# Roots of a norm made token by token, and one accumulated read of a state, in a two-layer decoder step

## The reference, cut to what matters

```python
def rms_norm(x, gain=None):
    y = x * lax.rsqrt(jnp.mean(x * x, axis=-1, keepdims=True) + EPS)
    return y * gain

def decoder_layer(x, ...):
    h = x + 0.5 * rms_norm(swiglu(rms_norm(x, n_ffn1_pre), ffn1_w_in, ffn1_w_out), n_ffn1_post)
    m, ... = token_mixing(rms_norm(h, n_mix_pre), ...)
    h = h + rms_norm(m, n_mix_post)
    h = h + 0.5 * rms_norm(swiglu(rms_norm(h, n_ffn2_pre), ffn2_w_in, ffn2_w_out), n_ffn2_post)
```

## Time and profile before

| what | value |
|---|---|
| median of 3 runs | 1864.43 us (1863.88 to 1865.13) |
| profiled execution, own time | 1863.31 us |
| its span, first to last instruction | 1861.5 us |
| PE busy | 1810.6 us, 97% |
| DVE busy | 1344.2 us, 72% |
| ACT busy | 902.9 us, 49% |
| POOL busy | 118.5 us, 6% |
| chain that ended last | PE 71%, DVE 16%, issue 5%, ACT 4%, DMA 2% |
| DMA | 368.20 MB, mean 198 GB/s |

### The profile page before, as it was taken

One profiled execution on the slowest core, in us unless ns is written; L12 is line 12 of the kernel. 1 busy time (PEld: TensorE's weight loads), 2 busy tenths in 40 slices (PEclk: granted clock), 3 DMA queues, 4 the chain that ended last, 5 costly groups with the idle time before them and its releaser, 6 DMA issues.

```text
span 1861.5 us, 40412 instructions
## 1 busy us (share of the span) xinstructions
PE 1810.6 (97%) x16247; PEld 1746.6 (94%) x16247; DVE 1344.2 (72%) x2096; ACT 902.9 (49%) x1051; POOL 118.5 (6%) x174
## 2 busy tenths in 40 slices
PE   7999999999999999999999999999999899999998
PEld 6999999988989999999999999999889899989998
DVE  6777577787777868877577765868777776887764
ACT  5443354546574254543354434465567545354433
POOL 0000001111210100000000000010112010000000
PEclk9999999999999999999999999999999999999999
DMA  7776666766864656566667766676778465546654
GB/s 231 216 206 192 178 196 221 237 226 216 276 227 139 192 169 220 162 191 168 173 188 212 205 184 198 198 247 201 232 235 283 138 205 170 181 129 189 182 163 133
DMA packets 433619, 368.20 MB, mean 198 GB/s; under 512 B 9395, under 2 KB 411125, under 8 KB 432811
## 3 DMA queue, kind: packets, MB, share of 16 engines
q1 hardware_dynamic: 409560, 276.60, 50.0%
q0 software_dynamic: 23872, 89.03, 14.2%
HBM read 338.90 MB, written 26.69 MB: 196 GB/s over the span
## 4 chain that ended last, share of the span: by engine, by line
PE 71%; DVE 16%; issue 5%; ACT 4%; DMA 2%; DVEq 0%; SPq 0%; ACTq 0%
PE proj L686 46%; PE proj L709 4%; PE proj L704 4%; PE proj L705 4%; DVE wl L1859 3%; ACT wh L1364 2%; PE aux L749 1%; PE proj L660 1%; PE aux L919 1%; PE aux L1141 1%; PE aux L864 1%; PE aux L880 1%; DVE y L2053 1%; DVE x L2054 1%; DMA raw<-w_mem_v 1%
## 5 line engine op out<-in xcount | busy, mean ns | idle before, releaser
L1859 DVE TENSOR_TENSOR wl<-raw,wh 128x2048 fp32r<-128x2048 f32 (+1 forms) x280 | 599.2, 2140 | 193.2 <-ACT wh L1364 167.9
L1364 ACT CAST wh<-raw 128x2048 fp32r<-128x2048 f32 (+1 forms) x280 | 500.3, 1787 | 249.3 <-PE proj L686 105.9
L686 PE MATMUL proj<-xl,wh 128*128 128x264 f32 x2624 | 381.4, 286 | 1.9 <-DVEq L2009 1.3
L686 PE MATMUL proj<-xh,wh 128*128 128x264 f32 x2624 | 380.1, 287 | 0.0
L686 PE MATMUL proj<-xh,wl 128*128 128x264 f32 x2624 | 372.0, 284 | 1.8 <-DVE wl L1859 1.1
L686 PEld LDWEIGHTS proj<-xl,wh 128*128 128x128 f32 x2624 | 341.3, 188 | 15.5 <-issue 13.2
L686 PEld LDWEIGHTS proj<-xh,wl 128*128 128x128 f32 x2624 | 339.0, 188 | 4.2 <-DVE wl L1859 3.9
L686 PEld LDWEIGHTS proj<-xh,wh 128*128 128x128 f32 x2624 | 340.0, 188 | 3.1 <-issue 0.8
L705 PE MATMUL proj<-hl,wh 128*128 128x264 f32 x704 | 173.3, 283 | 0.0
L704 PE MATMUL proj<-hh,wh 128*128 128x264 f32 x704 | 173.0, 283 | 0.0
L1385 ACT ACTIVATE gate<-gate 128x264 f32<-128x264 f32 x88 | 37.4, 425 | 246.2 <-DVEq L1895 246.2
(11 more groups left out here) (477 smaller groups left out, 2271.5 us busy)
## 6 DMA issues: line engine op xcount, KB each, us to landing
raw<-ffn_w_in SPq DMA_DIRECT2D x176, 512.0 KB, 5.1
raw<-w_in SPq DMA_DIRECT2D x80, 1024.0 KB, 5.6
raw<-ffn_w_out SPq DMA_DIRECT2D x64, 704.0 KB, 4.6
sring<-cache_mem_k POOLq DMA_DIRECT2D x32, 512.0 KB, 5.1
sring<-cache_mem_v POOLq DMA_DIRECT2D x32, 512.0 KB, 4.0
out<-sring POOLq DMA_DIRECT2D x32, 512.0 KB, 4.5
sring<-state_gdn POOLq DMA_DIRECT2D x30, 512.0 KB, 5.1
raw<-w_mem_v SPq DMA_DIRECT2D x8, 1024.0 KB, 6.9
```

What stands on the lines that cost most here:

```text
L686: mm = pe.matmul(o, w[:, s, k * 256 + t * P:k * 256 + (t + 1) * P], a[:, k, :], **go)
L1364: act.copy(wh[:, slot, 0:size], raw[:, slot, 0:size]).then_inc(hi_done[slot], 1)
L1859: dve.tensor_sub(wl[:, slot, 0:size], raw[:, slot, 0:size], wh[:, slot, 0:size].bitcast(F32)).then_inc(split_done[slot], 1)
```

## The change

At three places (layer 0 after `out`, layer 0 after `f2o`, layer 1 after `out`) the sums of squares are made with `acc` as the stationary operand, 128 tokens at a time, against one column of ones: the sum of a token then stands in that token's partition, three tokens a partition. ScalarE takes the roots of 128x3 values, VectorE inverts them and announces `row_roots`. Between that and the multiplications of `y` VectorE does the split that stood in front of `add_result` (only in layer 0's two places). TensorE spreads the three columns over all partitions with three matmuls against the identity, and VectorE multiplies `y` with the roots straight from PSUM.

The delta rule's reads: the stationary operand `gqm` has 128 columns a sample, zero but for the columns of that sample, so that the products of all eight samples add up in one bank (`gd`), which VectorE copies once. TensorE itself releases the states' slots. With it `rn1` moves behind the sixth matmul of the second tile of group 1, and from banks 0 and 1 to 2 and 3; `gQ0` and `gQ1` move from bank 1 to 2; `query_part(1)` moves behind `o_ret`.

```diff
@@ banks, in the order of use
-         + ["gvn1", "gd0", "rn0", "rn1", "gd1", "gbr0", "gG0", "gQ0", "gd2", "gbr1", "gG1", "gQ1", "gd3", "gT"]
+         + ["gvn1", "gd", "rn0", "rn1", "gbr0", "gG0", "gQ0", "gbr1", "gG1", "gQ1", "gT"]
-              "spt": 2, "gvn0": 0, "rd7": 2, "rS6": 0, "rS7": 2, "rdt": 0, "gqd": 1, "gvn1": 2, "gd0": 1, "rn1": 0, "gd1": 2, "gbr0": 0, "gG0": 3, "gQ0": 1,
-              "gd2": 2, "gbr1": 0, "gG1": 3, "gQ1": 1, "gd3": 2, "gT": 0}
+              "spt": 2, "gvn0": 0, "rd7": 2, "rS6": 0, "rS7": 2, "rdt": 0, "gqd": 1, "gvn1": 2, "gd": 1, "rn1": 2, "gbr0": 0, "gG0": 3, "gQ0": 2,
+              "gbr1": 0, "gG1": 3, "gQ1": 2, "gT": 0}
@@ TensorE
+            ENDS = (0, P, T - P)
+            def row_sums(l, name):
+                norm_wait(pe, l, "sqp", int(name[1]))
                 o = begin(l, name)
+                for c, first in enumerate(ENDS):
+                    mm = pe.matmul(o[:, 0, c:c + 1], acc[:, first:first + P], ones[:, 0:1], start=True, stop=True)
+                end(mm, name)
+            def spread_roots(l, n):
+                pe.wait_ge(M["row_roots"], 2 * l + n - 1)
+                o = begin(l, f"r{n}")
+                for c, (first, width) in enumerate(((0, P), (P, P), (SEQ, NS))):
+                    mm = pe.matmul(o[:, 0, first:first + width], mx[:, c:c + 1].broadcast_to([P, P]), ident[:, P - width:P], start=True, stop=True)
+                end(mm, f"r{n}")
...
                 def last_result(g):
                     if l and g == 0:
-                        total(l - 1, "p3", "sqp")
+                        row_sums(l - 1, "p3")
+                def last_roots(g, t, k):
+                    if l and (g, t, k) == (0, 1, 3):
+                        spread_roots(l - 1, 3)
...
                 def read_delta(g, t, k):
+                    if (g, t, k) == (1, 1, 1):
+                        retention_sums(1)
                     if (t, k) != (1, 3):
                         return
-                    o = begin(l, f"gd{g}")
-                    for c in range(2):
-                        unit_wait(pe, l, D_UNIT + 2 * g + c)
-                        mm = four_heads(o[:, 0, c * DV:(c + 1) * DV], lambda h: gqw[:, h, :], delta_unit(2 * g + c), start=True, stop=True)
-                    end(mm, f"gd{g}")
+                    o = begin(l, "gd") if g == 0 else aux[:, PLACE["gd"][0]:PLACE["gd"][0] + 1, :]
+                    for b in (2 * g, 2 * g + 1):
+                        slot = unit_wait(pe, l, D_UNIT + b)
+                        mm = four_heads(o[:, 0, 0:DV], lambda h: gqm[:, b * P + h * 32:b * P + (h + 1) * 32], delta_unit(b),
+                                        start=(b == 0), stop=(b == NS - 1))
...
                     elif g == 1:
                         second("rsq", 1)
-                        for s in range(2):
-                            o = begin(l, f"rn{s}")
...
+                        retention_sums(0)
...
                 else:
                     mixed_result(0)
-                    keep_streaming(l, "n3", 22)
+                    o = begin(l, "n3")
+                    keep_streaming(o, 4)
+                    spread_roots(l, 2)
+                    keep_streaming(o, 11)
@@ ScalarE
+            def row_root(l, name):
+                o = take(act, l, name)
+                order(act.activation(mx[:, 0:3], o[:, 0, 0:3], ACT.Sqrt, bias=epst[:], scale=1.0 / D))
+                release(act, name)
+                act.sem_inc(M["rtp"], 1)
@@ VectorE
-                def add_result(n):
+                def add_result(n, between=None):
                     norm_wait(dve, l, "rtp", n)
-                    order(dve.reciprocal(rt[:], rt[:]))
+                    if n == 1:
+                        root = rt[:]
+                        order(dve.reciprocal(root, root))
+                    else:
+                        order(dve.reciprocal(mx[:, 0:3], mx[:, 0:3]))
+                        tell("row_roots")
+                        if between:
+                            between()
+                        root = take(dve, l, f"r{n}")[:, 0, 0:T]
...
                     elif g in (2, 3):
                         z = g - 2
+                        if g == 2:
+                            ready("rS_out")
+                            order(dve.memset(gqm[:], 0.0))
...
-                        order(cp(gqw[:].rearrange("p h (c n) -> p c h n", c=2), qkvt[:, 0:8, T - 16:T].rearrange("p (c h) n -> p c h n", c=2)))
+                        last = (NS - 1) * (P + 1)
+                        for c in range(2):
+                            own_columns = gqm[:, 0:last].rearrange("p (b j) -> p b j", j=P + 1)[:, :, NS + 16 * c:P:32]
+                            order.apart(cp(own_columns.rearrange("p b h -> p h b"), qkvt[:, 4 * c:4 * c + 4, SEQ:T - 1]))
+                            order.apart(cp(gqm[:, last + NS + 16 * c::32], qkvt[:, 4 * c:4 * c + 4, T - 1]))
+                        order.wait()
...
-                def read_delta(k):
-
-                    o = take(dve, l, f"gd{k}")[:, 0, :]
-                    for c in range(2):
-                        own_part(accd, o[:, c * DV:(c + 1) * DV], own_row, 2 * k + c)
-                    release(dve, f"gd{k}")
...
+                def keep_delta_reads():
+                    order(cp(accd[:], take(dve, l, "gd")[:, 0, 0:DV]))
+                    release(dve, "gd")
+                    dve.sem_inc(unit_used[(D_UNIT + NS - 1) % SRING], 1)
+                    tell("reads")
...
                 def finish_retention(g, remainder=None):
-                    if g < 3:
-                        read_delta(g)
...
-                        read_delta(3)
-                        query_part(1)
+                        keep_delta_reads()
                 def gate_retention(g):
                     if g == 3:
...
                         tell("o_ret")
+                        query_part(1)
```

More of the change, by code:

```diff
@@ L98 @@
          + ["gv0", "gx4", "gS0", "go0", "gks", "gx5", "gv1", "gx6", "go1", "gS1", "gx7", "gm0", "gm1"]
-         + ["p2", "n3", "q3", "p3"])
-ONE_BANK = ("gbr0 gbr1 n1 n2 n3 q1 q2 q3 p1 p2 p3 gaw gab smt spt rks gcs rqd gcol gev gqd gkS gmt svt rdt gdt gT gw0 gw1 mqs0 mqs1 mqs2 mqs3 "
-            + " ".join(f"{n}{k}" for n in ("sp", "rd", "gd", "sv") for k in range(2 * NS)) + " "
+         + ["p2", "r2", "n3", "q3", "p3", "r3"])
+ONE_BANK = ("gbr0 gbr1 n1 n2 n3 q1 q2 q3 r2 r3 p1 p2 p3 gaw gab smt spt rks gcs rqd gcol gev gqd gd gkS gmt svt rdt gdt gT gw0 gw1 mqs0 mqs1 mqs2 mqs3 "
+            + " ".join(f"{n}{k}" for n in ("sp", "rd", "sv") for k in range(2 * NS)) + " "
             + " ".join(f"{n}{s}" for n in ("gG", "gQ") + tuple(f"{n}{g}" for n in ("gy", "gt") for g in range(LEVELS)) for s in range(2)) + " " + " ".join(f"{n}{g}" for n in ("gc", "gu") for g in range(SMALL))).split()
@@ L1072, in _, with retention_sums @@
                 products(l, "x2", (xh, xl), (oh, ol), "mix", branch="o_mem", after=prepare_delta, mid=update_retention, inner=read_retention)
+                def retention_sums(s):
+                    o = begin(l, f"rn{s}")
+                    for hd in range(2):
+                        mm = pe.matmul(o[:, hd, 0:T], ones[:], rsq[:, 2 * s + hd, :], start=True, stop=True)
+                    end(mm, f"rn{s}")
                 def read_delta(g, t, k):
+                    if (g, t, k) == (1, 1, 1):
+                        retention_sums(1)
                     if (t, k) != (1, 3):
                         return
-                    o = begin(l, f"gd{g}")
-                    for c in range(2):
-                        unit_wait(pe, l, D_UNIT + 2 * g + c)
-                        mm = four_heads(o[:, 0, c * DV:(c + 1) * DV], lambda h: gqw[:, h, :], delta_unit(2 * g + c), start=True, stop=True)
-                    end(mm, f"gd{g}")
+                    o = begin(l, "gd") if g == 0 else aux[:, PLACE["gd"][0]:PLACE["gd"][0] + 1, :]
[3 more added lines that the diff above has]
+                                        start=(b == 0), stop=(b == NS - 1))
+                        if b == NS - 1:
+                            end(mm, "gd")
+                        else:
+                            mm.then_inc(unit_used[slot], 1)
                 def blocks(o, left, right):
@@ L1119, in turn_keys @@
                         second("rsq", 1)
-                        for s in range(2):
-                            o = begin(l, f"rn{s}")
-                            for hd in range(2):
-                                mm = pe.matmul(o[:, hd, 0:T], ones[:], rsq[:, 2 * s + hd, :], start=True, stop=True)
-                            end(mm, f"rn{s}")
+                        retention_sums(0)
                     elif g == 3:
@@ L1511, in values @@
                     return copied(l, lambda g, t: mvn[:, t, (g + first) * 256:(g + first + 1) * 256],
-                                  mid=lambda g: root(*result, "rtp") if result and g == 0 else None)
```

(9 more changed lines are left out.)

31 lines of the change are left out of this document (17 added, 14 removed).

## The result

The changed kernel takes 1868.31 us in the median of 22 runs (1866.04 to 1872.86), the kernel before 1864.83 us (1862.90 to 1872.67, 22 runs on the same chip). The ratio is 1.0016, with a 95% interval of 1.0010 to 1.0022: slower by 3.0 us by the ratio and by 3.5 us between the medians. The forecast was 1863.1 us with a range up to 1866.9, so it missed, and with it the sign. The profiled execution took 1870.17 us, its span is 1868.4 us.

A forecast was written before the change was run, and what follows sets the result against it. TensorE, busy for 97% of the span, was taken as the bound. Roots -0.85 us and reads -0.5 us sum to -1.35 us: 1861.96 us profiled, 1863.1 us on the median, with a range of 1859.6 to 1866.9 us.

The forecast's parts named there:

- The memset: Stage `x2`, VectorE: clearing 1024 columns costs nothing, as 3.08 us of idle time follow; without that cover 0.9 us.
- The bank that moves: `rn1` on the banks of `rn0`: TensorE waits 2.1 us for ScalarE, and `gbr0` comes 1.7 us late.
- What the shorter chain gives back: Stage `rg` to `oh`: VectorE's saved reads remove old waits, one ahead of `gkS` appears; gain 0.25 us per layer.
- The roots: Three places where a result's root is made: three-column sums and roots, then spreading; -0.85 us in all.
- Layer 1: After `out`, nothing else in the chain: `y` starts near 1650.65 in place of 1651.50, gain 0.8 us.
- Layer 0: After `out`, split now behind the reciprocal: `y` starts at 743.9 in place of 744.36, gain 0.45 us.
- Between the layers: The root is late and the split now follows it: `y` at 953.65 in place of 953.25, loss 0.4 us.
- Rival B: TensorE's clock falls in four new waits, 1.7 us each; three give 1868.2 us; chance 0.14 (one, two), 0.08 (three, four).
- the reads' part: The sibling's reads, with the moved bank and the shorter VectorE chain, over both layers: -0.5 us.

## Why the prediction was wrong

**The memset (the step that failed first).** The prediction priced it at nothing, because 3.08 us of idle time follow in `x2`. They do, but some 15 us later (481.48 against the memset at 466.06). In between stands the copy that frees a bank, and TensorE's `rd3` wants that bank at once: 1.05 and 0.68 us of wait, forecast 0, of which 0.8 and 0.46 us still stand at `rd4`. Its fall-back, "if that cover were gone it would be the 0.9 us", had the size and not the reason: the cover was never at that place.

**The bank that moves.** The wait at `rn1` was forecast at 2.1 us and is 1.66. The delay at `gbr0`, 1.7 us forecast, is 7.77 - 5.93 = 1.84 us, measured from `rn0`. No wait at `gT` and `gdt`, and one of over 2 us ahead of `gkS`: right. So was the claim that the wait at `rn1` comes out of old waits and doesn't reach `oh` (removed, `gkS` starts no earlier).

**What the shorter chain gives back.** Forecast -0.25 us per layer at `oh`, measured from `rn0` +0.47 in layer 0 and +0.08 in layer 1 (38.75 against 38.67). `gkS` started at 557.43, 38.51 us after `rn0`, and 38.40 in layer 1, forecast 38.1. From there to `oh` the prediction allowed 0.35 us; layer 1 has it, and layer 0 took 0.67 us at the lowered clock (0.36 with the waits filled). So the mechanism was right, VectorE's chain was 0.3 to 0.4 us longer than its sum, and the rest of layer 0 is the clock. What the prediction did not ask is whether `gkS` has to stand there; moving it is worth some 2 us per layer at `oh`.

**The roots.** Layer 1: `y` starts 2.44 us after the sums in every profile where the clock is whole there, 3.22 before, so 0.78 against a forecast 0.8. In the first profile of the changed kernel it is 3.55; the clock had fallen there, and so it had where it is 3.08, with `gkS` alone moved. Layer 0: `y` starts 5.35 us after the last addition to `acc` before, 4.49 in the changed kernel and 4.77 with the roots alone, so 0.6 to 0.9 us given back, forecast 0.45; in three other profiles with the split behind the reciprocal it is 5.5 to 5.9, so this gain is not a steady one. Between the layers: forecast a loss of 0.4 us. From ScalarE's root to `y` it is 2.94 us in place of 2.46 in all kernels with the split behind, a loss of 0.5. Counted from the start of the cast of the weight group before that, it is 11.96 us with the roots alone in place of 10.90, a loss of 1.1; but this stretch is 10.1 to 11.2 us in the kernels with the old roots and 10.1 to 12.9 in those with the new and the split behind. The prediction took ScalarE's root from the row of before. But ScalarE's table load stands behind a cast that waits for weights, 0.35 us before, 1.37 in the changed kernel, 1.32 with the roots alone, 2.46 with the steps and the memset moved (0.81 with the steps alone): in that stage an earlier kernel may only wait longer for the weights' arrival. That is a reading; no run holds the arrival fixed.

**Rival B.** Its mechanism exists (falls follow the new waits, and fillers remove them), its number with three falls, 1868.2 us, fits the median to 0.1 us by luck, and it is not the cause. At equal mean clock the difference stays 3.5 us.
The Trainium skill ("TensorE: Matmul & The Clock Gate", "HAM oscillation — how this bites in real kernels") has a kernel pay for the clock's fall again at each wait between bursts. The runs agree in part for a single kernel: on the same occasion, filling the waits takes the mean clock from 0.9976 to 0.9993 and the time from 1864.99 to 1859.02 us. But not each wait has its fall: behind the 1.5 to 1.7 us at `rn1` the clock stayed whole in every profile that has this wait. And the rule can't be used for this change, since the kernel before pays as much already.

**The sum, corrected.** From `rd0` to `oh`, the stretch that holds all of the reads' part, the changed kernel takes 113.80 us in place of 112.54 in layer 0 and 113.05 in place of 112.29 in layer 1: +2.0 us, 1.3 of it the memset as seen at `rd4`, where the forecast was -0.5. The roots come to -0.8 - 0.6 + 1.1 = -0.3. Together +1.7 us against a measured +3.0 to +3.5. Of the forecast's error of some 4.5 us, the memset is 1.3 to 1.7, the rest of the reads' part 0.8 to 1.2, the place between the layers 0.7. Some 1.5 us stay unplaced; so does part of the gap of 4 to 6 us between the unfilled and the filled kernels, of which the mean clock, 0.0011 to 0.0018 of 1865 us, explains 2 to 3.4. A candidate is the arrival of weights between the layers, which varied from profile to profile by 1 to 3 us; no run here holds it fixed.

## What to carry to other kernels

An idle stretch covers only what stands in it: before an added instruction is priced at nothing, read who waits for the very next thing on its engine, not how much idle time the stage has. Where several waits of one engine lead to the same late result, removing the first moves it to the later ones (here 1.66 us at `rn1`, with nothing gained); look instead for what stands in the queue ahead of the late result and isn't urgent itself. And compare the clock of two kernels over all timed runs, never over two profiles.

## What was not expected of the hardware

- The same instructions with the same waits met a whole and a lowered clock in different executions. After `out` of layer 1, behind a wait of 1.12 us, PEclk was 0.66 in one profile, and with the roots alone and with the steps moved the same sequence ran at full speed (eight filler records in 1.14 us against 1.74). The row with the roots alone:
```profile
1650.08 1.14 PE L735 MATMUL aux<-ones,ident 128*128 128x128 f32 x8
```
- Over the 120 runs the kernel before spans 0.994 to 0.999 in mean clock, and 1868.22 to 1863.92 us with it: about 0.9 us per 0.001, half of what 0.001 of 1865 us is.
- Ten unneeded fp32 products of 128x128 in the waits of layer 0 and twenty-one in those of layer 1 raised the mean clock from 0.9976 to 0.9993 and went with the fastest time. In the kernel before, such products raised it from 0.9969 to 0.9980 and gained nothing.
